# Strassen MLP of a hybrid encoder: down products moved one block behind the up products, operands made in place, sides of u contiguous

## What is computed

```
x = x + jnp.square(jax.nn.relu(_rmsnorm(x, g_mlp) @ w_up)) @ w_down     # w_up 1024x4096, w_down 4096x1024
```

## Time and profile before

| | us |
|---|---|
| median of 3 runs | 3212.96 |
| the profiled execution, its own time | 3209.45 |
| its span, first to last instruction | 3207.6 |
| PE matmul busy | 2885.8 (90%) |
| DVE busy | 1832.5 (57%) |
| ACT busy | 910.4 (28%) |
| POOL busy | 423.4 (13%) |
| mean granted TensorE clock | 0.921 of full |

### The profile page before, as it was taken

The page is one execution under the profiler, slowest core; times in us unless marked ns, Lnnn a source line. Parts: engine busy times, 40 slices in busy tenths (PEclk is TensorE's granted clock), DMA queues, the critical chain, the costliest instruction groups (busy, mean ns, idle before and its releaser), DMA issues. The chain is left out here.

```text
span 3207.6 us, 42512 instructions
## 1 busy us (share of the span) xinstructions
PE 2885.8 (90%) x15015; PEld 2490.5 (78%) x15015; DVE 1832.5 (57%) x2992; ACT 910.4 (28%) x1914; POOL 423.4 (13%) x401
## 2 busy tenths in 40 slices
PE   7999998999997789998899888888898888887998
PEld 6888886788885778887789777777887777775887
DVE  7676765545543556656565556556545555555443
ACT  4333333333332322222222222222212222222332
POOL 0000000000000311111122211211301111110110
PEclk9999998999999599999996999999679998998999
DMA  4221115333322311121123211212302111114221
GB/s 171 70 69 51 63 58 135 127 107 108 108 97 75 122 53 52 61 64 59 52 65 119 78 53 56 75 52 63 118 27 63 61 59 52 52 52 153 81 82 45
DMA packets 165592, 249.30 MB, mean 78 GB/s; under 512 B 12104, under 2 KB 115624, under 8 KB 165512
## 3 DMA queue, kind: packets, MB, share of 16 engines
q1 hardware_dynamic: 163160, 239.71, 23.2%
q0 software_dynamic: 2352, 8.52, 0.7%
HBM read 191.34 MB, written 56.95 MB: 77 GB/s over the span
## 5 line engine op out<-in xcount | busy, mean ns | idle before, releaser
L97 PE MATMUL f_down<-f_down_hi,f_uT_hi 128*128 128x512 f32 (+1 forms) x1088 | 472.5, 434 | 178.0 <-DVE f_uT_lo L1823 168.5
L97 PE MATMUL f_up<-f_op_hi,f_up_hi 128*128 128x384 f32 (+5 forms) x1540 | 519.7, 337 | 67.2 <-DVE f_op_lo L1801 38.2
L98 PE MATMUL f_up<-f_op_lo,f_up_hi 128*128 128x384 f32 (+5 forms) x1540 | 516.7, 336 | 0.0
L99 PE MATMUL f_up<-f_op_hi,f_up_lo 128*128 128x384 f32 (+5 forms) x1540 | 516.6, 335 | 0.0
L1831 DVE TENSOR_TENSOR f_acc<-f_acc,f_down 128x1024 f32<-128x1024 f32 (+1 forms) x272 | 331.8, 1220 | 322.6 <-PE f_down L99 322.6
L98 PE MATMUL f_down<-f_down_lo,f_uT_hi 128*128 128x512 f32 (+1 forms) x1088 | 464.3, 427 | 0.0
L99 PE MATMUL f_down<-f_down_hi,f_uT_lo 128*128 128x512 f32 (+1 forms) x1088 | 462.1, 425 | 0.0
L97 PEld LDWEIGHTS f_down<-f_down_hi,f_uT_hi 128*128 128x128 f32 (+1 forms) x1088 | 227.0, 209 | 244.2 <-issue 190.7
L97 PEld LDWEIGHTS f_up<-f_op_hi,f_up_hi 128*128 128x128 f32 x1540 | 329.0, 214 | 80.1 <-DVE f_op_lo L1801 39.9
L98 PEld LDWEIGHTS f_up<-f_op_lo,f_up_hi 128*128 128x128 f32 x1540 | 329.4, 214 | 2.0
L99 PEld LDWEIGHTS f_up<-f_op_hi,f_up_lo 128*128 128x128 f32 x1540 | 329.5, 214 | 0.0
(11 more groups left out here) (319 smaller groups left out, 5206.0 us busy)
## 6 DMA issues: line engine op xcount, KB each, us to landing
f_up_raw<-in_w_up SPq DMA_DIRECT2D x96, 512.0 KB, 5.4
f_down_raw<-in_w_down SPq DMA_DIRECT2D x96, 512.0 KB, 4.4
hT_hi_kept<-m_hT_hi SPq DMA_DIRECT2D x17, 512.0 KB, 4.9
hT_lo_kept<-m_hT_lo SPq DMA_DIRECT2D x17, 512.0 KB, 5.7
a_hT_hi<-hT_hi_kept SPq DMA_DIRECT2D x17, 512.0 KB, 3.7
a_hT_lo<-hT_lo_kept SPq DMA_DIRECT2D x17, 512.0 KB, 4.5
m_x<-in_x_prompt SPq DMA_DIRECT2D x16, 512.0 KB, 4.2
a_x_sum<-in_x_prompt SPq DMA_DIRECT2D x16, 512.0 KB, 6.6
```

What stands on the lines that cost most here:

```text
L97: eng.matmul(out, lh(k), rh(k), start=f, stop=False)
L98: eng.matmul(out, lh(k), rl(k), start=False, stop=False)
L99: ins = eng.matmul(out, ll(k), rh(k), start=False, stop=e)
```

## The change

The down products of block b-1 are issued behind the up products of block b; in the last block of a pass the down products of blocks 14 and 15 follow each other. Both down weights are split at the head of a block, ahead of `take_p1` and of the combines. `u_half` now waits for `down_done`, since `uT` is still the u of the block before. Only pass 0 runs block 0 by units. The operands of the next pass are made in the last block of a pass, among its adds, and `stage` writes its results over `h`. The paired tiles' u lie in contiguous halves of `uT` (side 0, then side 1); single tiles still interleave, so a quarter of u is written in two pieces in passes 1 and 2.

```
-    OPERANDS = [B11, T1, T2, B21, B22, T3, T4]
+    OPERANDS = [B11, B22, B21, T1, T3, T2, T4]
-        uT_hi, uT_lo = sb("uT_hi", [P, 2, WIDTH, 2], F32R), sb("uT_lo", [P, 2, WIDTH, 2], F32R)
+        uT_hi, uT_lo = sb("uT_hi", [P, 2, 2 * WIDTH], F32R), sb("uT_lo", [P, 2, 2 * WIDTH], F32R)
         def tiles(p):
-            return sorted(i for unit in UNITS[p] for i in unit)
+            pairs = [unit for unit in UNITS[p] if len(unit) == 2]
+            return [a for a, _ in pairs] + [unit[0] for unit in UNITS[p] if len(unit) == 1] + [b for _, b in pairs]
...
         @block.sync                                          # body(b), b >= 1
+                    ahead = place_of(b - 1, 1)
                     if not final:
                         reached(sp, up_lo_made, g * 7 + 7)
-                        load_up(nxt)
-                    reached(sp, down_lo_made, g * 2 + 1)
-                    load_down(places[1])
+                        load_up(after)
+                    reached(sp, down_lo_made, g * 2 - 1)
+                    load_down(ahead)
+                    reached(sp, down_lo_made, g * 2)
+                    load_down(here[0])
...
         @block.gpsimd                                        # stage
-                pool.tensor_tensor(t1_buf(w), b12, b11, ALU.subtract).then_inc(staged, 1)
-                pool.wait_ge(staged, number * 4 + 1)
-                pool.tensor_tensor(t2_buf(w), b22, t1_buf(w), ALU.subtract).then_inc(staged, 1)
+                pool.wait_ge(op_lo, number * 7 + 1)
+                pool.tensor_tensor(b11, b12, b11, ALU.subtract).then_inc(staged, 1)
                 pool.tensor_tensor(b12, b22, b12, ALU.subtract).then_inc(staged, 1)
...
         @block.scalar                                        # body(b), b >= 1
+                    for f in (0, 1):
+                        down_weight_hi(p, b - 1, f)
+                    take_p1(k, cols.stop - cols.start)
+                    ahead = ready(p, b + 1) if not last else ready_pass(p + 1) if p < PASSES[-1] else iter(())
+                    for _ in range(4 if not last else AHEAD):
+                        next(ahead, None)
+                    for n in (0, 1):
+                        u_half(p, b, k, cols, n)
+                    for _ in range(3 if not last else AHEAD):
+                        next(ahead, None)
+                    for n in (2, 3):
+                        u_half(p, b, k, cols, n)
+                    if last:
+                        for f in (0, 1):
+                            down_weight_hi(p, b, f)
                         whole(ahead)
...
         @block.tensor                                        # body(b)
-                    down(p, b)
+                    if not is_block(b, 0):
+                        down(p, b - 1)
+                    if is_block(b, BLOCKS - 1):
+                        down(p, b)
...
         @block.vector                                        # body(b), b >= 1
+                    for f in (0, 1):
+                        down_weight_lo(p, b - 1, f)
+                    chain(k, cols.stop - cols.start, iter(()))
+                    for n, i in enumerate(tiles(p)):
+                        add(p, b - 1, n, i)
...
+                    if last:
+                        for f in (0, 1):
+                            down_weight_lo(p, b, f)
+                        for n, i in enumerate(tiles(p)):
+                            add(p, b, n, i)
+                            for _ in range(3):
+                                next(ahead, None)
                         whole(ahead)
```

More of the change, by code:

```diff
@@ L1497, in groups @@
         def groups(p, b):
-            return [unit_cols(p, u) for u in range(len(UNITS[p]))] if isinstance(b, int) and b == 0 else [all_cols(p)]
+            if p == 0 and isinstance(b, int) and b == 0:
+                return [unit_cols(p, u) for u in range(len(UNITS[p]))]
+            return [all_cols(p)]
         def group_count(p, b):
[L1501 to L1504, removed]
+            ahead = len(UNITS[0]) - 1
+            if p == 0 and isinstance(b, int) and b == 0:
+                return 0
+            return b + (p * BLOCKS + ahead)
         def last_group(p, b):
@@ L1701, in down_weight_hi, with u_half @@
                 act.activation(down_hi[:, f], down_raw[:], ACT.Copy).then_inc(down_hi_made, 1)
[L1703 to L1707, removed]
+            def u_half(p, b, k, cols, n):
+                quarter = U_ORDER[n]
+                f, side = QUARTERS[quarter]
+                reached(act, squared, k * 4 + quarter + 1)
+                if not is_block(b, 0):
+                    reached(act, down_done, down_count(p, b - 1, side0_done(p) if n < 2 else len(tiles(p)) - 1))
+                for out, at in u_parts(uT_hi, p, f, side, cols):
+                    ins = act.activation(out, part[:, PART_OF[quarter], at], ACT.Copy)
+                ins.then_inc(u_hi, 1)
             def take_p1(k, w):
@@ L1720, in body @@
                 def body(b):
[L1721 to L1749, removed]
-                            next(ahead)
+                    first, last = is_block(b, 0), is_block(b, BLOCKS - 1)
+                    if first:
+                        for u, cols in enumerate(groups(p, b)):
+                            k, w = group_count(p, b) + u, cols.stop - cols.start
+                            units = u + 1 < len(groups(p, b))
+                            ahead = operands_hi(p, u + 1) if units else ready(p, 1)
+                            next(ahead)
+                            next(ahead)
+                            take_p1(k, w)
+                            for _ in range(4):
+                                next(ahead)
+                            for n in range(4):
+                                u_half(p, b, k, cols, n)
+                            whole(ahead)
+                        return
@@ L1884, in body @@
-                    crossing = last and p < PASSES[-1]
-                    ahead = operands_lo(p + 1, 0) if crossing else iter(range(7))
-                    weights = 0
-                    for n, i in enumerate(tiles(p)):
-                        if n == len(tiles(p)) - 1:
-                            while weights < 7 and not (last and not crossing):
-                                up_weight_lo(*((p + 1, 0) if crossing else (p, b + 1)), weights)
-                                weights += 1
-                                if weights > 1:
-                                    next(ahead)
-                            whole(ahead)
-                        add(p, b, n, i)
-                        if n < len(tiles(p)) - 2 and not (last and not crossing):
-                            up_weight_lo(*((p + 1, 0) if crossing else (p, b + 1)), weights)
-                            weights += 1
-                            if weights > 1:
-                                next(ahead)
+                    first, last = is_block(b, 0), is_block(b, BLOCKS - 1)
@@ new lines, in body @@
+                    if first:
+                        for u, cols in enumerate(groups(p, b)):
+                            k, w = group_count(p, b) + u, cols.stop - cols.start
+                            units = u + 1 < len(groups(p, b))
+                            ahead = operands_lo(p, u + 1) if units else ready(p, 1)
+                            next(ahead)
+                            next(ahead)
+                            chain(k, w, ahead)
+                            for n in range(4):
+                                u_low(p, k, cols, n)
+                            whole(ahead)
+                        return
@@ new lines, in body @@
+                    k, cols = group_count(p, b), all_cols(p)
+                    for f in (0, 1):
+                        down_weight_lo(p, b - 1, f)
+                    chain(k, cols.stop - cols.start, iter(()))
+                    ahead = ready(p, b + 1) if not last else ready_pass(p + 1) if p < PASSES[-1] else iter(())
+                    half, count = side0_done(p), len(tiles(p))
+                    for n, i in enumerate(tiles(p)):
+                        add(p, b - 1, n, i)
+                        if n < half:
+                            items = shared(AHEAD if last else 4, half, n)
+                        elif n > half:
+                            items = shared(AHEAD if last else 3, count - 1 - half, n - half - 1)
+                        else:
+                            items = 0
+                            for m in (0, 1):
+                                u_low(p, k, cols, m)
+                        for _ in range(items):
+                            next(ahead, None)
```

207 lines of the change are left out of this document (127 added, 80 removed).

## The result

The changed kernel took 3070.1 us, median of 4 runs (3066.8 to 3071.2), against 3215.4 before (3211.0 to 3219.5): ratio 0.9547, 95% interval 0.9530 to 0.9563. The forecast was 3056, in a range of 2985 to 3115. The profiled execution took 3070.38 us with a span of 3068.4.

The account below looks back on a forecast made before the run. PE was taken as the bound. Passes of 604.0, 530.9 and 569.1 us sum to 1704.0 against 1861.4, 157.4 less; from 3209.45 that gives 3052, plus 3.5 for the median: 3056 us, range 2985 to 3115.

Parts of the forecast that it names:

- What is late next: Steady block: the second down weight (f = 1), requested at S+4.3, arrives late, and take_p1, needed by product 4, waits behind it.
- S+10.9: Pass 0 steady block: take_p1 done 10.9 us after S, the end of the down products of block b-2.
- the stall: Mid-up in each steady block, PE waits at products 4 and 5: 2.6, 4.2 and 3.8 us in passes 0, 1, 2.
- The clock term of pass 0: Time lost to a lower granted clock after the mid-up stall: 0.8 us a block in pass 0.
- The rival without a new stall: f = 1 arrives in time for product 4, so no mid-up stall and no clock loss: 2831 us, chance 0.06.
- down(14): Down products of block 14: 1.4 us longer, as DVE has weights and operands between its adds; 17.8 and 15.0 us.
- D to the next pass: From D, the end of down(14), through the stall and down(15) to the next pass: 31.6 and 35.5 us.
- last turn of pass 2: Block 15 of pass 2: up products, down(14), a 10.3 us stall and the last down products, together 64.1 us.
- Pass 0 keeps its 55.0: Pass 0's head: the unit-by-unit up products of block 0 still take 55.0 us.
- The handover stalls: Between the down products of blocks 14 and 15, PE stands about 11 us; 10.3 us in pass 2.
- Contiguous u: Paired tiles' u without a step shortens down matmuls from 0.233 to 0.227 us, about 0.4 us a pass 0 block.
- the rule cited there: Skill note on 16-byte SBUF cachelines: a two-float32 step keeps full bandwidth, so contiguous u gains nothing; result 16 us later.

Follow-up runs that it names:

- p1_first: Changed kernel with take_p1 between the two down weights on ACT and the f = 1 `lo` behind the first square on DVE: 2849.4 us, ratio 0.8871.
- half_loads: Changed kernel without the loads of the second down weight, f = 1 being split from the rows loaded for f = 0: 2824.2 us, ratio 0.8790.
- the ninth run: p1_first with five next-pass operands between block 15's down weights, and the unit's seventh operand made before the chain's last combine: 2838.9 us, ratio 0.8827.

## Why the prediction was right, and where it was off

The steps on the loop held. What is late next (the load of f = 1, with `take_p1` behind it), its time (S+10.9), the stall (2.6, 4.2 and 3.8 us forecast; 2.6, 3.8 to 4.1 and 3.4 to 3.8 measured), the down phases of 16.4, 13.6 and 16.4 us (16.5, 13.8, 16.6) and the periods came out within 0.1 us. The clock term of pass 0 was too dear, 0.8 us where the 15 blocks averaged 0.4 (3 of them lose 1.8); in passes 1 and 2 it averaged 2.1 and 1.8 against 1.8. That pass 0 came out at 34.4 all the same is luck: its blocks without a dip take 34.0 us, 3.0 more than p1_first's 30.95, so the stall costs 0.4 us more than the 2.6 of the sum, and the two errors cancel. Two readings were wrong without harm. PE reaches product 4 at S+0.2+8.35 = 8.55, not 8.4 (8.5 measured). And DVE was not busy half the time or less before, but 60% of pass 0 (381.6 of 632.2 us); it is one of the two queues in which the new wait arose. The rival without a new stall is what p1_first and half_loads make of the kernel; here it wasn't so.

The loops came to 1317.1 us against 1316.9. The miss of 14 us in the MLP lies at the ends of the passes:

| us | forecast | measured |
|---|---|---|
| pass 0 to the end of block 1's turn | 89.4 | 93.1 |
| pass 1 and pass 2, the same | 46.0, 51.3 | 46.4, 52.4 |
| up products of block 15, passes 0 and 1 | 18.0, 18.4 | 17.8, 20.2 |
| down(14), passes 0 and 1 | 17.8, 15.0 | 21.0, 18.3 |
| D to the next pass | 31.6, 35.5 | 33.6, 38.2 |
| last turn of pass 2 (up, down, stall, down) | 64.1 | 60.0 |

- "Pass 0 keeps its 55.0" failed: that head took 58.9 us. The seventh operand's `lo` now stands behind the `u_low` of the unit before, and PE waits twice 2.29 us for it; the ninth run removed exactly that.
- Down(14) was mis-sized by 3.2 us. I gave DVE 1.4 us for the `lo`s between its adds; in pass 0 PE waits 2.30 and 1.65 us for adds, in pass 1 2.30 us, and the matmuls behind that dip in clock (0.91 over the phase). Ahead of the adds in question three of DVE's 128x512 subtractions took 1.77 us, where their neighbours took 0.68, two ahead of the first and one ahead of the second. Each began while POOL was in a subtraction of its own. That POOL slows them is what these rows suggest; no run took POOL's work away:

```profile
1629.61 1.78 DVE L1864 TENSOR_TENSOR f_op_lo<-f_h,f_op_hi 128x512 fp32r<-128x512 f32 x1
1631.32 1.77 DVE L1869 TENSOR_TENSOR f_up_lo<-f_sums,f_up_hi 128x512 fp32r<-128x512 f32 x1
1633.01 1.21 DVE L1896 TENSOR_TENSOR f_acc<-f_acc,f_down 128x1024 f32<-128x1024 f32 x1
...
1634.74 0.68 DVE L1869 TENSOR_TENSOR f_up_lo<-f_sums,f_up_hi 128x512 fp32r<-128x512 f32 x1
1635.35 1.77 DVE L1864 TENSOR_TENSOR f_op_lo<-f_h,f_op_hi 128x512 fp32r<-128x512 f32 x1
1637.05 0.68 DVE L1869 TENSOR_TENSOR f_up_lo<-f_up_raw,f_up_hi 128x512 fp32r<-128x512 f32 x1
1637.65 1.21 DVE L1896 TENSOR_TENSOR f_acc<-f_acc,f_down 128x1024 f32<-128x1024 f32 x1
...
1629.24 1.61 POOL L1676 TENSOR_TENSOR f_h<-f_h 128x512 f32<-128x512 f32 x1 [8.64 <-DVE f_op_lo L1864]
1630.80 1.74 POOL L1677 TENSOR_TENSOR f_h<-f_h 128x512 f32<-128x512 f32 x1
1634.97 1.60 POOL L1683 TENSOR_TENSOR f_h<-f_h 128x512 f32<-128x512 f32 x1 [0.74 <-DVE f_op_lo L1864]
```

- The handover stalls held (11 and 11.4 us forecast; 10.2 and 11.6), as did their cause, the load; what follows them was 2 to 3 us longer. In pass 2's last block, where no up weights are loaded, the stall in mid-up is only 1.9 us, and the 36 matmuls behind it kept full clock; the last stall is 9.4 us, not 10.3. Together the turn is 4.1 us less than forecast.
- Contiguous u held: the sum's 0.4 us for a block of pass 0 was 0.44, and its price could be read from two neighbouring tiles, against the rule cited there.
- Staging in place, costed at nothing, cost nothing that shows: PE stands 29.8 us ahead of the first up product, 30.2 before.

## What to carry to other kernels

When a wait is removed, follow each engine's queue in order to what is late next: an instruction that needs nothing of a load still waits for it if it stands behind one that does, and here the order of two rows on each of two engines was worth 221 us, more than the 145 us of the change itself. Move such rows on every engine that PE waits for: on ACT alone nothing was won. Where the granted clock moves, a small gain can't be read from the whole time; ask for it in a version in which the clock stays up. And read a matmul's price together with its granted clock.

## What was not expected of the hardware

- A stall of 2.6 us cost clock in 3 of 15 blocks in one kernel and in 11 of 15 in another; those of 3.4 to 5.8 us cost it in all 29 blocks of passes 1 and 2 that have them.
- After a wait of 9.8 us the full-width matmuls of pass 2's head ran at a mean clock of 0.94, but the narrow ones in the same place stayed at 1.2 GHz, without a gap between them, until 5 us into the full-width ones that follow: 77 us. There matmuls of 128, 64 and 16 columns all took 0.213 us. In pass 1 of the same run the clock fell from 2.4 to 1.2 GHz 4 us into the 64-column matmuls, with no wait ahead of it.
- Down matmuls whose stationary operand is read with a step of two words take 0.235 us instead of 0.229, at full clock.
